# Packing the products of the 8 sample rows into four 32-column groups of the PE array, in a hybrid decoder step

## Chip, cores and metric

One Trainium2 chip, one core. The metric is the device time of one launch in microseconds; runs of the same kernel are compared by their median. TensorE is called PE below, VectorE DVE, ScalarE ACT, GpSimd POOL, and SyncE, which issues nearly all DMAs from one queue, SP.

## What is computed

One layer of a causal decoder for a prompt of 1024 rows (`x_prompt`) and a group of 8 sample rows (`x_sample`, one token of each of 8 sequences at position 8192), with the same weights:

```
h  = LN_in(x)
z  = h @ W_in -> retention q,k,v,gate | dilated-attention q,k,v      (1024 x 3584)
m  = concat(swish(gate) * HeadNorm(Retention(q,k,v)), DilatedAttn(q,k,v)) @ W_out
h1 = LN1(alpha * h + m)
f  = up-projection -> causal depthwise conv (width 3) -> a * gelu(g) -> down-projection
e  = sigmoid(h1 @ W_pg) * (p @ W_pp)
h  = LN2(alpha * h1 + f + e)
```

There are 8 heads of 64 in the retention and 8 of 64 in the attention. A prompt row attends to the prompt under three bands (128, 512 by 4, 2048 by 16). A sample row uses its own cache of 2048 keys and values and its own retention state. The new keys and values, the states and the last up-projected rows are outputs too. Everything is fp32 outside; inside, large products split each operand into an fp16 high part and an fp16 remainder and add three of the four partial products (`PASSES`: high by high, high by low, low by high).

## The kernel before

The program is a row of stages, each with one instruction stream for each engine and semaphores between them: norm_in, retention, attention, samples, mixer, ffn. A stage ends for all engines together, and the next starts after it. The order of the work on each engine is the order in which the code of its stream is written. The prompt has 8 tiles of 128 rows (`t`, `NT` = 8), and the sample rows are a ninth, short tile; `HT` holds the transposed rows in both halves, [128, 2, 8, 1032], with the samples in the last 8 columns. `product` (L80) runs the 3 x 8 matmuls of one output of 512 columns: the rows are the stationary operand, the weights stream.

**retention**: for each pair of heads `p` (4) nine steps `s`, of which the ninth (`s == NT`) is the samples'. PE's step projects tile `s` (L441), then does for older tiles, one to four steps behind, the transposes of q and k (L450), scores (L458), the state, scores by values and the new state (L470 to L474, in one PSUM bank, OB) and the transpose of the result (L479). DVE turns the pairs of the projected tile (`turn_pairs`, L530), and, for the tile three steps behind, updates the state, norms OB (L594) and multiplies by the gate (L598). L470 of a tile waits until L594 of the tile before has read OB. At odd steps DVE also splits weights for the next pair. The loop over the middle pairs is a hardware loop.

**attention**: written out, `g` counts 4 x 9 steps. PE: `project(g)` (L784), `turn(g-1)`, `score(g-2)`, `values(g-5)` (L829). ACT: `soften(g)`, which for the tile three steps back holds two exponentials and two scalings (L847, L855), `split` (L879), `out` (L905), `copy(g)` (L891: the projected tile from PSUM to `QKV`), `turned_high(g-1)`. POOL rotates `QKV` after the copy. SP, for each g: stores of tile g-1 after POOL's rotation (for the samples also to `scratch`), at some steps weight loads, then two DMA transposes of the normed scores (L721) for the tile three steps back. PE's `values` waits for these.

```
    for g in range(NG + LP + 2):
        p, s = divmod(g, NT + 1)
        store(g - 1)
        ...
                load_w(p, c)
        ...
        turn_p(g)
```

**samples**: DVE multiplies queries and cached keys, and a softmax over heads and rows follows, while PE mixes the first 6 tiles of the prompt with W_out (`mix`, through L84). Then PE weighs the cached values: for each of 8 samples b and 3 patterns one fp32 matmul (L1219), with `PBD` [128, 64] as stationary operand, which is zero outside the 8 columns of sample b, so that all 24 add up in one bank, OPS [64, 512]. DVE takes each row's own head out of it (`OWN`), and the result is turned into `MTS`, the samples' mixed rows. The values of a sample have one of four slots; SP loads the next sample into a slot when its three matmuls are done (`v_free`). Half of mix(5) stands between samples 3 and 4, half behind the last.

**mixer**: PE mixes the last two tiles of the prompt and the samples (`mix(2, 0, NB, 0)`, 48 matmuls), then for each of nine tiles turns the rows, runs the gate product (`gate`, 48 matmuls, L84 with `mixer_WG`) and the embedding product (`embed`, 12). ACT and DVE split the ten weight chunks of the gate and the embedding as they arrive; the gate needs eight of them. DVE's `add(t)` (L1482, L1486) finishes a tile.

**ffn**: up-projection, convolution, gelu, down-projection. The samples' part of the down-projection is packed already (`sample_parts`, L1697): the stationary operand holds both halves of the 8 rows, 16 columns, and goes to columns 0, 32, 64 and 96 of the array in turn, for two chunks with the high and the low weights each; the four column groups land in four groups of 32 rows of PSUM, and one matmul with the 0/1 matrix `SUMS` adds them up.

## Time and profile before

| | |
|---|---|
| median of 3 runs | 1564.14 us (1563.77 to 1565.64) |
| the profiled execution, device time | 1564.13 us |
| its span | 1562.3 us |
| PE busy | 1436.7 us (92%) |
| DVE busy | 800.6 us (51%) |
| ACT busy | 457.7 us (29%) |
| POOL busy | 265.9 us (17%) |
| mean granted clock of TensorE | 0.976 |

The profile is of one execution. Its span runs from the first to the last record; times in it are counted from its start. Busy time of an engine is the union of its instructions. A matmul's end is modelled, so the distance from start to start is what one costs in a stream, not the 379 ns given as its mean. An fp32 matmul leaves two records. The stages start at about 70 us (retention), 332 (attention), 574 (samples), 671 (mixer) and 838 (ffn).

### The profile page before, as it was taken

The numbers are of one execution on the slowest core, as the hardware profiler recorded it, in microseconds if no ns is written. First come the engines' busy times: TensorE is split into PE (matmuls) and PEld (weight loads), VectorE is DVE, ScalarE is ACT, GpSimd is POOL, SyncE is SP. The second block draws the span as 40 slices with busy tenths as digits, with TensorE's granted clock in tenths as the row PEclk, the third lists the DMA queues.
The fourth block names the chain that finished last, engine by engine and source line by source line (L and its number), as shares of the span: only waits on it lengthen the run. The fifth ranks groups of instructions, "written<-read, shape, count | busy, mean of one in ns | idle before, by whom it ended". The sixth has DMA issues, their size and how long they took to land. (4 is left out here: it accounts for less than half of the span.)

```text
span 1562.3 us, 24517 instructions
## 1 busy us (share of the span) xinstructions
PE 1436.7 (92%) x8964; PEld 810.6 (52%) x8964; DVE 800.6 (51%) x1611; ACT 457.7 (29%) x743; POOL 265.9 (17%) x330
## 2 busy tenths in 40 slices
PE   1599999969999958999998999999999999999986
PEld 1355555545555533344544666456654566546643
DVE  6656766637567648167533445125541355413547
ACT  2321221127556630022111443004440144302322
POOL 3400101123333305012210110001110011100026
PEclk9999999979999978999999999999999999999998
DMA  7101010026687778341005122012120122101002
GB/s 207 57 27 42 18 50 28 14 60 123 120 156 144 149 164 244 128 148 59 11 1 147 49 78 81 0 40 74 59 69 0 40 81 81 40 0 41 14 14 101
DMA packets 184281, 115.64 MB, mean 74 GB/s; under 512 B 83239, under 2 KB 168055, under 8 KB 183943
## 3 DMA queue, kind: packets, MB, share of 16 engines
q1 hardware_dynamic: 184207, 114.66, 28.3%
q8 instruction: 45, 0.74, 0.2%
q14 instruction: 29, 0.24, 0.0%
HBM read 85.79 MB, written 10.15 MB: 61 GB/s over the span
## 5 line engine op out<-in xcount | busy, mean ns | idle before, releaser
L1647 PE MATMUL PS<-all_HT,all_WS 128*128 128x344 f16 x3168 | 465.1, 310 | 6.5 <-POOLq L73 4.8
L1647 PEld LDWEIGHTS PS<-all_HT,all_WS 128*128 128x128 f16 x3168 | 310.5, 98 | 161.7 <-issue 8.4
L441 PE MATMUL PS<-all_WS,all_HT 128*128 (+3 forms) x864 | 194.4, 382 | 3.8 <-POOLq L73 3.8
L1657 PE MATMUL PS<-all_WS,ffn_HG 128*128 128x512 f16 x608 | 182.3, 379 | 3.6 <-POOL ffn_HG L1807 1.9
L1807 POOL TENSOR_TENSOR ffn_HG<-ffn_PRD,ffn_HG 128x1032 f32 (+1 forms) x22 | 47.2, 2146 | 660.0 <-ACT ffn_HG L1779 660.0
L1767 ACT ACTIVATE ffn_C<-PS,all_CW,all_CWS 128x1032 f32<-128x1032 f32 x44 | 53.1, 1206 | 362.0 <-PE PS L1647 362.0
L784 PE MATMUL PS<-all_WS,all_HT 128*128 128x384 f16 (+1 forms) x864 | 149.2, 330 | 2.9 <-POOLq L73 2.9
L441 PEld LDWEIGHTS PS<-all_WS,all_HT 128*128 128x128 f16 (+1 forms) x864 | 83.7, 97 | 101.3 <-POOLq L73 3.9
L1657 PE MATMUL PS<-ffn_WD,ffn_HG 128*128 128x512 f16 x304 | 115.2, 379 | 0.0
L784 PEld LDWEIGHTS PS<-all_WS,all_HT 128*128 128x128 f16 (+1 forms) x864 | 81.6, 98 | 61.5 <-POOLq L73 3.2
L1657 PEld LDWEIGHTS PS<-all_WS,ffn_HG 128*128 (+1 forms) x608 | 59.4, 98 | 76.9 <-issue 6.0
L84 PE MATMUL PS<-all_WS,all_MT 128*128 128x512 f16 x384 | 88.2, 392 | 11.0 <-DVE all_HRES L1135 7.4
L1864 DVE SCALAR_TENSOR_TENSOR all_HRES<-PS,all_HRES 128x1024 f32 x24 | 29.4, 1225 | 129.1 <-PE PS L1657 128.8
L84 PE MATMUL PS<-mixer_WG,all_HT 128*128 128x512 f16 (+1 forms) x432 | 94.7, 379 | 0.0
L1833 DVE SCALAR_TENSOR_TENSOR all_WS<-ffn_SU,all_WS 128x2048 f16<-128x2048 f32 x21 | 52.0, 2478 | 66.2 <-ACT all_WS L1757 66.2
L1843 DVE TENSOR_SCALAR ffn_UC<-PS 128x10 f32 (+1 forms) x44 | 7.6, 172 | 147.1 <-ACT ffn_CB L1768 147.1
L84 PEld LDWEIGHTS PS<-all_WS,all_MT 128*128 128x128 f16 x384 | 38.1, 100 | 60.3 <-issue 11.2
L84 PEld LDWEIGHTS PS<-mixer_WG,all_HT 128*128 128x128 f16 (+1 forms) x432 | 41.6, 97 | 49.9 <-issue 0.4
L606 POOL TENSOR_TENSOR retention_RSTD<-retention_VE,all_EPSC 128x2 f32<-128x2 f32 x32 | 24.8, 774 | 240.3 <-DVE retention_VE L579 240.3
L847 ACT ACTIVATE attention_PR<-attention_PR,attention_MX 128x128 f32<-128x128 f32 (+7 forms) x64 | 49.1, 767 | 41.2 <-DVE attention_MX L924 41.1
L281 PE MATMUL PS<-all_IDENT,norm_in_HS 128*128 128x128 f32 (+1 forms) x72 | 16.7, 407 | 47.6 <-POOL norm_in_HS L261 47.6
L493 ACT ACTIVATE retention_V<-PS 128x128 f32<-128x128 f32 x32 | 8.9, 278 | 173.0 <-DVE retention_T L530 173.0
(210 smaller groups left out, 1862.9 us busy)
## 6 DMA issues: line engine op xcount, KB each, us to landing
ffn_SU<-in_w_up SPq DMA_DIRECT2D x42, 512.0 KB, 5.0
ffn_SD<-in_w_down SPq DMA_DIRECT2D x22, 512.0 KB, 3.5
all_STG<-in_w_in SPq DMA_DIRECT2D x32, 256.0 KB, 3.2
all_STG<-in_w_in SPq DMA_DIRECT2D x32, 192.0 KB, 3.0
samples_KC<-in_cache_k_win SPq DMA_DIRECT2D x24, 256.0 KB, 3.9
all_HRES<-in_x_prompt SPq DMA_DIRECT2D x8, 512.0 KB, 4.9
out<-attention_QKV SPq DMA_DIRECT2D x64, 64.0 KB, 1.7
all_STG<-in_w_out SPq DMA_DIRECT2D x8, 512.0 KB, 4.0
```

What stands on the lines that cost most here:

```text
L84: mm = nc.tensor.matmul(out[:n], lhs(a, k), w(b, k, c), start=(k == 0 and (a, b) == (0, 0)), stop=(k == kd - 1 and (a, b) == (1, 0)))
L281: last = nc.tensor.transpose(PS[:, 2 * u + k // 4, (k % 4) * P:(k % 4) * P + n], HS[:n, u, k * P:(k + 1) * P], IDENT[:n, :n])
L441: mm = nc.tensor.matmul(Z(s)[:n], HT[:, a, k, s * P:s * P + n], WS[:, slot, b, k, :], start=(k == 0 and (a, b) == (0, 0)), stop=(k == KD - ...
L606: nc.gpsimd.tensor_tensor(RSTD[:], VE[:], EPSC[:], ALU.pow).then_inc(rstd_ready, 1)
L784: mm = nc.tensor.matmul(Z[:n, g % 2, 0:384], HT[:, a, k, s * P:s * P + n], WS[:, p % 2, b, k, 0:384], start=(k == 0 and (a, b) == (0, 0)), ...
L847: nc.scalar.activation(PR[:, x % 4, 0:w], PR[:, x % 4, 0:w], ACT.Exp, scale=-1.0, bias=MX[:, x % 4:x % 4 + 1], accum_out=SUM[:, x % 4:x % ...
L1647: mm = nc.tensor.matmul(U(x)[:, third], UW[:, u, a, k, x * P:(x + 1) * P], HT[:, b, k, third * T3:(third + 1) * T3], start=(k == 0 and (a, ...
L1657: mm = nc.tensor.matmul(DB[u][:rows, half], HG[:, a, l, ds(t * P, rows)], WD[b][:, l, half * 512:(half + 1) * 512], start=(l == 0 and (a, ...
L1767: nc.scalar.activation(C_from(x, 0), U(x), ACT.Identity, scale=CWS[:, 2, ch], bias=CW[:, 3, ch])
L1807: nc.gpsimd.tensor_tensor(HG[:, 1, l, :], PRD[:], HG[:, 0, l, :], ALU.subtract).then_inc(lo_ready, 1)
L1833: nc.vector.scalar_tensor_tensor(UW[:, u, 1].rearrange("p k n -> p (k n)"), SU[:, u].rearrange("p k n -> p (k n)"), S_W, UW[:, u, 0].rearr ...
L1864: nc.vector.scalar_tensor_tensor(HRES[:n, t], DB[u][:n].rearrange("p b n -> p (b n)"), UNDOWN, HRES[:n, t], ALU.mult, ALU.add).then_inc(ad ...
```

## The change

All products whose output rows are the 8 samples are done as ffn's already are: both halves of the rows side by side as a stationary operand of 16 columns (`HTS`, `MTS` in a new layout), two chunks times two halves of the weights in the four column groups at once, 16 matmuls in place of 24 (32 in place of 48); then ACT copies all 128 rows of the partial sums to SBUF and one fp32 matmul with `SUMS` (now loaded once, in norm_in) adds them up. The product of the low parts, which was left out, is thereby included. This holds for the projections in retention and attention, for the mixing and for the gate in the mixer stage. In samples, each of four samples has a column group of its own, with its own 8 probabilities as stationary operand (`PT`, no zeros), the halves of the eight go to two banks, and two small matmuls with a 0/1 matrix (`SEL`) choose the rows. All four slots are reloaded when the whole first half is done. The two helpers that ran retention's pairs in a hardware loop now write them out. In the mixer the gate's packed product stands before embed(7). `dynamic_dma_scratch_size` falls from 1024 to 512.

```diff
+        def product_parts(out, lhs, w, kd):
+            for r in range(kd // 2):
+                for j in range(4):
+                    mm = nc.tensor.matmul(out[32 * j:32 * j + 2 * NB], lhs(2 * r + j // 2), w(j % 2, 2 * r + j // 2),
+                                          start=(r == 0), stop=(r == kd // 2 - 1))
+            return mm
...
@@ norm_in: SP, DVE
+                    sp.dma_start(SUMS[:], c_sum).then_inc(tab_in, 16)
...
+                    dve.wait_ge(lo_ready, BASE + NT + 1)
+                    nc.vector.tensor_copy(HTS[:].rearrange("p k a n -> p a k n"), HT[:, :, :, SEQ:])
...
@@ retention: both loop helpers
-                    with eng.Fori(1, HP - 1) as p:
+                    for p in range(1, HP - 1):
...
@@ retention: PE
                                 if s == NT:
                                     pe.sem_inc(pe_go, 1)
-                                for k in range(KD):
...
+                                    pe.wait_ge(parts_zero, BASE + 1)
+                                    product_parts(Z(s), lambda k: HTS[:, k].rearrange("p a n -> p (a n)"),
+                                                  lambda b, k: WS[:, slot, b, k, :], KD).then_inc(z_parts, 1)
...
                                 nc.tensor.transpose(RB, R[:, t % 2], IDENT[:]).then_inc(r_turned, 1)
+                            if s == NT:
+                                pe.wait_ge(zp_ready, BASE + p + 1)
+                                nc.tensor.matmul(Z(s)[:NB], SUMS[:], ZP[:], start=True, stop=True).then_inc(z_ready, 1)
@@ retention: ACT
+                                if s == NT:
+                                    act.wait_ge(z_parts, BASE + p + 1)
+                                    nc.scalar.activation(ZP[:], Z(s), ACT.Copy).then_inc(zp_ready, 1)
                                 act.wait_ge(halves, BASE + 18 * p + 2 * s + 2)
@@ attention: PE
+                    def add_up(g):
+                        p, s = divmod(g, NT + 1)
+                        if s == NT and 0 <= g < NG:
+                            pe.wait_ge(zp_ready, BASE + p + 1)
+                            nc.tensor.matmul(Z[:NB, g % 2, 0:384], SUMS[:], QKV[:, g % 3], start=True, stop=True).then_inc(z_summed, 1)
...
                             project(g)
+                        add_up(g - 1)
                         turn(g - 1)
@@ attention: ACT
+                        if s == NT:
+                            nc.scalar.activation(QKV[:, g % 3], Z[:, g % 2, 0:384], ACT.Copy).then_inc(zp_ready, 1)
...
+                    def copy_sum(g):
+                        p, s = divmod(g, NT + 1)
+                        if s == NT and 0 <= g < NG:
+                            act.wait_ge(z_summed, BASE + p + 1)
+                            nc.scalar.activation(QKV[:NB, g % 3], Z[:NB, g % 2, 0:384], ACT.Copy, scale=UNSCALE).then_inc(copied, 1)
...
                         soften(g)
+                        copy_sum(g - 1)
                         split(g)
@@ samples: SP, PE, DVE
                         else:
-                            sp.wait_ge(v_free, BASE + b - 3)
+                            sp.wait_ge(pv_done, BASE + 1)
...
+                    def weigh(half):
+                        pe.wait_ge(pt_ready, BASE + 1)
+                        pe.wait_ge(bank_zero, BASE + half + 1)
+                        for j in range(4):
+                            pe.wait_ge(v_in[j], BASE + 48 * (half + 1))
                         for a in range(PAT):
+                            for j in range(4):
+                                b = 4 * half + j
+                                mm = nc.tensor.matmul(OPS[half][32 * j:32 * j + H], PT[:, a, b * H:(b + 1) * H], v_slot(b)[:, a],
+                                                      start=(a == 0), stop=(a == PAT - 1))
+                        mm.then_inc(pv_done, 1)
...
+                    weigh(0)
                     mix(5, (0,))
+                    weigh(1)
                     mix(5, (1,))
+                    pe.wait_ge(ao_ready, BASE + 1)
+                    for half in range(2):
+                        mm = nc.tensor.matmul(APS, SEL[:, half], AO[:, half], start=(half == 0), stop=(half == 1))
+                    mm.then_inc(chosen, 1)
...
+                    dve.wait_ge(chosen, BASE + 1)
                     for twice in range(2):
-                        nc.vector.scalar_tensor_tensor(MIX[:R8, 1, twice], ROW[:R8, 6], SR[:R8, PAT * P:], AO[:R8], ALU.mult,
+                        nc.vector.scalar_tensor_tensor(MIX[:R8, 1, twice], ROW[:R8, 6], SR[:R8, PAT * P:], APS, ALU.mult,
                                                        ALU.add).then_inc(att_done, 1)
@@ mixer: PE, ACT, DVE
                     mix(1, 1, P, (EARLY + 1) * P)
+                    pe.wait_ge(r_ready, BASE + 1)
+                    for c in range(2):
+                        mm = product_parts(M[0][:, c], lambda k: MTS[:, k].rearrange("p a n -> p (a n)"),
+                                           lambda b, k: WS[:, k // 4, b, 2 * (k % 4) + c], KD)
+                    mm.then_inc(parts_done, 1)
                     turn(0)
-                    mix(2, 0, NB, 0)
                     turn_p(0)
+                    add_up(M[0], 1).then_inc(mixed, 1)
...
+                        if t == NT - 1:
+                            gate_parts()
                         embed(t)
+                    add_up(TB, 2).then_inc(gated, 1)
+                    embed(NT)
...
                     for c in range(5, KD):
                         split(c)
+                    copy_parts(M[0], 1)
                     high_p(0)
...
                             low_p(t + 1)
+                        if t == NT - 1:
+                            dve.wait_ge(lo_ready, BASE + NT + 1)
+                            nc.vector.tensor_copy(HTS[:].rearrange("p k a n -> p a k n"), HT[:, :, :, SEQ:]).then_inc(hts_ready, 1)
                         add(t)
```

Two places in the order of the work, each before and after.

ACT in attention, from the sample tile (g = 8) to the next: before, the one copy of the 8 rows.

```order
L891 ACTIVATE attention_QKV<-PS 8x384 [waits attention_v_lo,attention_turned,attention_out_st2,attention_z_ready]
L899 ACTIVATE attention_QKT<-PS 128x256 [waits attention_turned]
L847 ACTIVATE attention_PR,attention_SUM<-attention_PR,attention_MX 128x896 [waits attention_masked]
L855 ACTIVATE attention_P<-attention_PR,attention_RCP 128x768 [waits attention_p_turned3,attention_rcp_ready]
L847 ACTIVATE attention_PR,attention_SUM<-attention_PR,attention_MX 128x896 [waits attention_masked]
L855 ACTIVATE attention_P<-attention_PR,attention_RCP 128x896 [waits attention_p_turned0,attention_rcp_ready]
L905 ACTIVATE all_MT<-PS 128x512 [waits attention_o_ready]
```

The same stretch with the change:

```order
L927 ACTIVATE attention_QKV<-PS 128x384 [waits attention_v_lo,attention_turned,attention_out_st2,attention_z_ready]
L943 ACTIVATE attention_QKT<-PS 128x256 [waits attention_turned]
L883 ACTIVATE attention_PR,attention_SUM<-attention_PR,attention_MX 128x896 [waits attention_masked]
L891 ACTIVATE attention_P<-attention_PR,attention_RCP 128x768 [waits attention_p_turned3,attention_rcp_ready]
L883 ACTIVATE attention_PR,attention_SUM<-attention_PR,attention_MX 128x896 [waits attention_masked]
L891 ACTIVATE attention_P<-attention_PR,attention_RCP 128x896 [waits attention_p_turned0,attention_rcp_ready]
L935 ACTIVATE attention_QKV<-PS 8x384 [waits attention_z_summed]
L949 ACTIVATE all_MT<-PS 128x512 [waits attention_o_ready]
```

The copy of the finished 8 rows moved from the first place to behind the four operations on the scores; in the first place stands the copy of the partial sums.

SP in attention, from the sample tile's stores, with the change; the order is that of before:

```order
L734 DMA out<-attention_QKV 8x128 [waits attention_rotated]
L734 DMA out<-attention_QKV 8x128
L737 DMA scratch<-attention_QKV 8x3x128
L720 DMA all_STG<-in_w_in 128x3x128 [waits attention_w_free]
...
L746 DMA_TRANSPOSE attention_PRT<-attention_P 128x12x128 [waits attention_o_ready,attention_p_lo] x2
L731 DMA out<-attention_QKV 128x128 [waits attention_rotated]
L731 DMA out<-attention_QKV 128x128
L746 DMA_TRANSPOSE attention_PRT<-attention_P 128x14x128 [waits attention_o_ready,attention_p_lo] x2
```

The transposes of tiles 5 (12 blocks of 128) and 6 (14) stand behind the stores of the sample tile.

PE in retention, the sample step and the beginning of the next, before:

```order
L441 MATMUL PS<-all_WS,all_HT 8x512 x24
L450 MATMUL PS<-all_IDENT,retention_QK 128x128 x2
L458 MATMUL PS<-retention_QKT 128x128 x2
L470 MATMUL PS<-retention_STATE,retention_QG 128x128
L472 MATMUL PS<-retention_V,retention_SD 128x64 x2
L474 MATMUL PS<-retention_V,retention_KG 128x128
L479 MATMUL PS<-all_IDENT,retention_R 128x128
```

With the change:

```order
L99 MATMUL PS<-all_WS,all_HTS 16x512 x16
L468 MATMUL PS<-all_IDENT,retention_QK 128x128 x2
L476 MATMUL PS<-retention_QKT 128x128 x2
L488 MATMUL PS<-retention_STATE,retention_QG 128x128
L490 MATMUL PS<-retention_V,retention_SD 128x64 x2
L492 MATMUL PS<-retention_V,retention_KG 128x128
L497 MATMUL PS<-all_IDENT,retention_R 128x128
L500 MATMUL PS<-retention_ZP,all_SUMS 8x512
L459 MATMUL PS<-all_WS,all_HT 128x512 x24
```

The sample projection has 16 matmuls in place of 24, and the finished rows exist only after L500, at the step's end.

## Rows read from the trace of the kernel before

**Rows 1.** Lines of PE: line, operation, shapes, count, busy us, mean ns, idle before.

```profile
L784 PE MATMUL PS<-all_WS,all_HT 128*8 128x384 f16 x96 | 16.3, 326 | 0.0
...
L1219 PE MATMUL PS<-samples_VC,samples_PRD 128*64 128x512 f32 x24 | 10.7, 595 | 0.0
```

**Rows 2.** Timeline of PE, ffn's packed product: start us, length us, instruction.

```profile
1029.02 0.38 PE L1697 MATMUL PS<-all_WS,ffn_HGS 128*16 128x512 f16 x1
...
1029.24 0.38 PE L1697 MATMUL PS<-all_WS,ffn_HGS 128*16 128x512 f16 x1
```

**Rows 3.** Timelines of PE and DVE, retention's first sample step.

```profile
124.10 5.34 PE L441 MATMUL PS<-all_WS,all_HT 128*8 128x512 f16 x24
...
130.16 0.49 PE L470 MATMUL PS<-retention_STATE,retention_QG 128*128 128x128 f32 x2
...
131.27 4.05 PE L441 MATMUL PS<-all_WS,all_HT 128*128 x18
...
127.60 0.58 DVE L594 TENSOR_SCALAR retention_RN<-PS,retention_MV,retention_RSTD 128x64 f32<-128x64 f32 x2
```

**Rows 4.** Timeline of PE, samples: the mixing after its longest wait.

```profile
602.27 23.34 PE L84 MATMUL PS<-all_WS,all_MT 128*128 128x512 f16 x96 [7.35 <-DVE all_HRES L1135]
```

**Rows 5.** Timeline of PE, attention: values of tile 4, then of tile 7 twice.

```profile
385.94 1.03 PE L829 MATMUL PS<-attention_PRT,all_WS 128*64 128x128 f16 x30 [0.25 <-DVE all_MT L978]
...
405.85 2.77 PE L829 MATMUL PS<-attention_PRT,all_WS 128*64 128x128 f16 x48 [3.08 <-issue]
...
461.51 1.53 PE L829 MATMUL PS<-attention_PRT,attention_V 128*64 128x128 f16 x48 [2.06 <-issue]
```

**Rows 6.** Timeline of ACT, attention, around the first sample tile.

```profile
377.92 0.48 ACT L891 ACTIVATE attention_QKV<-PS 8x384 f32<-8x384 f32 x1
...
384.50 0.58 ACT L905 ACTIVATE all_MT<-PS 128x512 f16<-128x512 f32 x1
```

**Rows 7.** Timeline of SP's queue, from the first sample tile's store to tile 7.

```profile
379.99 1.03 SPq L709 DMA_DIRECT2D out<-attention_QKV  x2
...
383.62 4.03 SPq L721 DMA_TRANSPOSE attention_PRT<-attention_P  x2
387.69 1.26 SPq L706 DMA_DIRECT2D out<-attention_QKV  x2
389.51 4.97 SPq L721 DMA_TRANSPOSE attention_PRT<-attention_P  x2
395.08 0.81 SPq L706 DMA_DIRECT2D out<-attention_QKV  x2
...
397.00 7.15 SPq L721 DMA_TRANSPOSE attention_PRT<-attention_P  x2
```

**Rows 8.** Samples: timelines of PE and SP; a window (engines' busy, PEclk, DMA share, GB/s).

```profile
637.37 5.32 PE L1219 MATMUL PS<-samples_VC,samples_PRD 128*64 128x512 f32 x12
...
663.72 5.34 PE L84 MATMUL PS<-all_WS,all_MT 128*128 128x512 f16 x24
...
640.14 3.85 SPq L1065 DMA_DIRECT2D samples_VC<-in_cache_v_win x6
...
655.00:656.00 1.00, 1.00 (x3) 0.27 (x2) 0.00 (x0) 0.00 (x0) 0.00 (x0) 1.00 0.23 90
```

**Rows 9.** Timeline of PE, retention: two transposes, then two fp32 matmuls in two row groups.

```profile
122.17 0.38 PE L450 MATMUL PS<-all_IDENT,retention_QK 128*128 128x128 f32 x2
122.48 0.49 PE L458 MATMUL PS<-retention_QKT 64*128 64x128 f32 x4
```

**Rows 10.** Mixer: timelines of ACT and PE at its start, of PE and DVE at its end.

```profile
702.53 1.06 ACT L1380 ACTIVATE mixer_WG<-mixer_STG 128x1024 f16<-128x1024 f32 x1 [3.02 <-DMA mixer_STG<-in_w_ple_gate]
...
708.37 10.52 PE L84 MATMUL PS<-mixer_WG,all_HT 128*128 128x512 f16 x48
...
819.84 10.52 PE L84 MATMUL PS<-mixer_WG,all_HT 128*8 128x512 f16 x48
...
834.24 1.21 DVE L1486 SCALAR_TENSOR_TENSOR all_HRES<-all_HRES,mixer_R 8x1024 f32<-8x1024 f32 x1
```

More of the change, by code:

```diff
@@ L369, in run @@
                 def run(eng):
-                    with eng.Fori(0, HP - 1) as p:
+                    for p in range(HP - 1):
                         body(eng, p, False)
@@ L1343, in gate, with gate_parts, add_up @@
                         for c in range(2):
-                            mm = product(GB[:, c], n, lambda a, k: HT[:, a, k, t * P:t * P + n],
+                            mm = product(GB[:, c], P, lambda a, k: HT[:, a, k, t * P:(t + 1) * P],
                                          lambda b, k, c: WG[:, b, k, c * 512:(c + 1) * 512], c, KD)
                         mm.then_inc(gated, 1)
+                    def gate_parts():
+                        pe.wait_ge(hts_ready, BASE + 1)
+                        for c in range(2):
+                            mm = product_parts(TB[:, c], lambda k: HTS[:, k].rearrange("p a n -> p (a n)"),
+                                               lambda b, k: WG[:, b, k, c * 512:(c + 1) * 512], KD)
+                        mm.then_inc(parts_done, 1)
+                    def add_up(out, count):
+                        pe.wait_ge(pp_ready, BASE + count)
+                        for c in range(2):
+                            mm = nc.tensor.matmul(out[:NB, c], SUMS[:], PP[:, c * 512:(c + 1) * 512], start=True, stop=True)
+                        return mm
                     def embed(t):
@@ L1961, in constants @@
     gsample = np.tile(np.exp(lg), NB)[:, None]
[L1962 removed]
+    own_head = np.tile(np.concatenate([np.eye(H), np.zeros((32 - H, H))]), (4, 1))
+    own_row = np.zeros((4, 32, 2, 2, 4, H))
+    for j in range(4):
+        for half in range(2):
+            own_row[j, :H, half, half, j] = np.eye(H)
+    own_row = own_row.reshape(P, 2 * NB * H)
     part_sum = np.tile(np.concatenate([np.eye(NB), np.eye(NB), np.zeros((2 * NB, NB))]), (4, 1))
     return [np.ascontiguousarray(a, dtype=f) for a in
[L1965 removed]
+            (np.eye(P), rope_ret, rope_att, decay, gq, kdec, gchunk, mask, gsample, own_head, part_sum, own_row)]
 _INS = ['x_prompt', 'x_sample', 'cache_k_win', 'cache_v_win', 'state_ret', 'state_conv', 'p_prompt', 'p_sample',
```

152 lines of the change are left out of this document (79 added, 73 removed).

## The prediction

> **What bounds the kernel now.** I read the view of windows first: TensorE (PE) is busy for nearly the whole of every stage, so removing PE time looks as if it paid one to one. The view of lines prices what is removed [rows 1]: a sample product of 24 matmuls, 8 rows each, takes as long as one of 128 rows, since a matmul costs its moving columns (16.3 us for the 96 of attention; 21.3 us for the 48 passes over the cached values, of which the row shows half). The question is then, at each of the five places, what ends the wait behind the removed work. For that I read the timelines of the engines around the sample block, and of SP's queue.
>
> **What a packed product costs.** The kernel has packed products already, in ffn [rows 2]: the row of 1029.02 is the first of four that start within 0.01 us, that of 1029.24 the first of the next four, 0.215 us later. So 16 matmuls of 512 columns take 4 x 0.215 = 0.86 us in place of 24 x 0.215 = 5.16, 16 of 384 columns 0.65 in place of 3.9, and 32 take 1.72 in place of 10.3. The new sum is one fp32 matmul over 512 columns: two passes of 10.7/24 = 0.44 us [rows 1], 0.87 together (0.65 for 384 columns). It stands behind a copy of ScalarE (ACT) of about 0.5 us.
>
> **Retention, four blocks.** The packed product is 4.3 us shorter, but DVE is not faster. In the block of sample rows PE next needs the OB bank, free once DVE has normed the tile before [rows 3]: 127.60 + 0.58 = 128.2. Now PE comes there at 130.16; after the change at 124.10 + 0.86 + 0.8 = 125.75, so it waits 2.5 us. From there 1.1 us to the end of the block (130.16 to 131.27, as now) and 0.87 for the sum: 130.3 in place of 131.27, 1.0 us gained. DVE gets the sample rows at 130.4 and not right behind the projection (124.10 + 5.34 = 129.4); the next tile's projection (5.2 us) covers that. Three blocks gain 2.9. The fourth has no projection behind it: the stage drains along DVE, which starts its sample rows 0.65 us later. Sum -2.2. The new waits of 2.5 us can lower PE's clock. After a wait of 7.35 us, 96 matmuls took 23.34 us [rows 4] and not 96 x 0.215 = 20.6, so a fall costs up to 2.7 us; after the wait of 2.06 us in [rows 5] the 48 matmuls took 1.53 us, as fast as elsewhere, after one of 3.08 us 2.77. I take one fall in three blocks, +2.0 (none: 0; all: 6). The unrolled loops add only code; PE shows no gap at the turns of the loop, so I cost them at nothing. **Retention: -0.2.**
>
> **Attention, four blocks.** Here two things eat the 3.9 - 0.65 - 0.65 = 2.6 us. First, PE's values of tile 4, one step after the sample block, wait already for ACT and DVE (0.25 us at 385.94 [rows 5]), whose chain of exponentials does not depend on the sample block. So PE only waits there for longer. Second, the finished sample rows come later, and SP stands in line behind them. Now ACT copies them at 377.92 [rows 6], GpSimd rotates them, and SP stores them at 379.99 [rows 7], 2.07 us after the copy began. With the change, that first copy only brings the partial sums; the second stands in ACT's order behind the four large operations of the next tile, which end at 384.50 [rows 6], 0.4 earlier at best. So SP's store starts at 384.1 + 2.07 = 386.2, +6.2 us. Behind that store in SP's order are the four weight loads and then the DMA transposes of tile 5. Those start at 383.62 now, with no pause since the store, and at 389.8 then. The pauses of SP after them, 388.95 to 389.51 and 395.89 - 0.81 - 394.48 = 0.6 us, are used up; the last pair (tile 7), at 397.00 now, starts 5.0 us later. PE's values of tile 7 wait for this pair even now: 3.08 us at 405.85, 2.06 at 461.51 [rows 5]. They come 5.0 us later in the first group; in the second and third I get +4.5 and +4.2 from the same steps, with the pauses that SP has there. PE runs without a gap from there to the next sample block, so nothing of it is regained. In the first group PE will have waited 4 us earlier (values of tile 5) and found its clock again by tile 7, where it is low now (2.77 us for the row at 405.85, 1.53 at 461.51): -1.9 with the projection behind it. The last group ends in a drain: ACT has the second copy (0.45 us) in its chain, and the last loads of W_out stand behind the late store; 0.5 to 2.5, taken as 1.5. **Attention: 3.1 + 4.5 + 4.2 + 1.5 = +13.3.** If SP caught up wholly it would be -5.5 (see the rivals); if PE's clock fell before the other tile 7s too, +17.
>
> **Cached values.** The 24 fp32 matmuls take 20.8 us from 637.37, with a half of mixing (5.2) in their middle and one at their end, from 663.72 [rows 8]. How do fp32 matmuls in different groups overlap? The trace has the question for groups of rows, [rows 9]: four passes of 128 columns (two matmuls) end 0.49 us after the first began, two passes after 0.38 with one step of 0.107. Four in sequence would need 0.38 + 2 x 0.107 = 0.59; 0.49 is one step fewer: the first pass of the second matmul runs beside the second pass of the first. So n matmuls take n + 1 passes, and 12 take 13 x 0.44 = 5.7 us in place of 10.4. But now a slot is refilled only when all four of the first half are done: loads start at 643.3, not at 640.14, and PE's second half waits for all twelve. Now 4.2 MB, 3.1 of them cached values, take from 641 to 655.7 [rows 8]: 11.9 us for the values, from issue. Second half at 655.2 (mixing hides 5.2 of that, 7 us stay bare), 5.7 us, 2.7 for the clock after such a wait, mixing 5.2, and a new tail: choosing matmuls and the two DVE operations on att_done now stand behind the mixing, 1.2 us. End 670.0, now 663.72 + 5.2 = 668.9. **+1.1.** Without any overlap (10.4 twice) it would be +10.5. The Trainium skill (TensorE: Matmul & The Clock Gate, Measured speedup vs the span model) gives packed matmuls one duration plus about 4 ns for each further tile. By that rule twelve would take three durations, 2.6 us, and this stage would give -5.1 (663.8); [rows 9] show another thing for fp32 with its two passes, and the sum goes by them.
>
> **Mixer.** At its start the sample product hides under the splitting of the gate weights: gate(0) needs eight, and ACT waits 3.02 us for DMA before the eighth, at 702.53 [rows 10]. PE turns the first tile only after the packed product, 1.8 us later than now, and ACT's and DVE's splits behind that move by 1.5. ACT's copy of the partial sums stands behind the eighth split, at 702.53 + 1.06 + 1.5 = 705.1; PE, idle for 9 us, adds at half clock (3.4 us) and reaches gate(0), with the turning of the next tile, at 711.0 in place of 708.37: +2.6. At the end there is nothing to hide behind: embed(7) ends at 819.84, and 10.4 for the gate, 2.6 for the embedding and DVE follow, up to 834.24 + 1.21 [rows 10]. After the change: 1.55 us of wait for the copy of HTS (DVE makes it only behind low_p), 1.8 for the packed gate, then embed(7), add_up 1.7, embed(8) 2.6 and DVE's 2.5: 830.0. -5.4. **-2.8.**
>
> norm_in's added copy and load end before ACT does, and ffn only loses a load. **Sum: -0.2 + 13.3 + 1.1 - 2.8 = +11.4.** The profiled execution took 1564.13 us, like the median of the runs (1564.14): **1575.5 us**. A measurement of this kernel tells 0.2% (3.1 us) from no change.
>
> **Rivals.**
> - *SP catches up.* Transposes take 7.15 us for the pair of tile 7 and 4.03 for that of tile 5 [rows 7], though four thirds as large. If the length comes from what else is under way, a queued pair may take 3 us; then tile 7 is served before 405.85, the waits of 3.08 and 2.06 us and the low clock (1.7) vanish, and attention gives -5.5: 1564.1 - 7.3 = **1556.8**. It decides from 5 us regained between the store and tile 7. Against it: the pairs get longer where loads and stores stand between them, and these stay. 0.21. If two thirds are regained, no change is measured: 0.12.
> - *All PE time counts:* four times 3.4 and 2.6, 9.4 at the cached values (20.8 - 11.4), 13.8 in the mixer, together -47: **1517**. It needs every wait above to be wrong. 0.05.
> - *fp32 groups side by side*, as the rule quoted: 6.2 us less than my sum, **1569.3**. Speaks for it: f16 does so. 0.12.
> - *fp32 groups one after another*, as column groups may differ from row groups: +9.4 on my sum, **1584.9**. 0.08.
>
> **Numbers.** My forecast has 0.42; with the last two rivals slower has 0.62, no change 0.12, faster 0.26. The range leaves out the second rival and part of the outermost: 1556 to 1585.
>
> **What would show it.** Right: SP's sample store 12 us after PE's sample block began and not 6; tile 5's transposes behind it; PE idle 4 us before the values of tile 5; ACT and DVE unchanged up to there; a wait of some 2.5 us at L470's successor in retention; some 7 us before the second half of the cached values; 9 us idle before the mixer's first sum. Wrong: values of tile 7 no later than now, or passes of fp32 groups that start together.

## The result, and the profile after

The changed kernel takes 1576.59 us (median of 4 runs, 1573.3 to 1576.87), the kernel before 1564.18 us in the same comparison: ratio 1.0080, 95% interval 1.0065 to 1.0094. It is slower by 12.4 us; 11.4 were forecast. The profiled execution has a span of 1574.5 us, 12.2 more than before. PE is busy for 1398.5 us, 38.2 us less than before: the removed work is gone, and the time is not.

Where the time came and went is read by stage. A stage starts with PE's first matmul in it; the table takes these starts from PE's timeline (70.34, 332.58, 574.04, 671.13 and 837.79 before; 69.80, 338.99, 596.79, 686.84 and 849.88 after).

| stage | before, us | after, us | difference | forecast |
|---|---|---|---|---|
| norm_in | 70.3 | 69.8 | -0.5 | 0 |
| retention | 262.2 | 269.2 | **+7.0** | -0.2 |
| attention | 241.5 | 257.8 | **+16.3** | +13.3 |
| samples | 97.1 | 90.1 | **-7.0** | +1.1 |
| mixer | 166.7 | 163.0 | -3.6 | -2.8 |
| ffn to the end | 724.5 | 724.6 | +0.1 | 0 |

So the total was right by luck, by errors of opposite sign: retention was underrated by 7.2 us, attention by 3.0, and samples overrated in cost by 8.1.

The view of windows of the changed kernel, retention, attention and samples; the columns are the stretch, its length, the busy time of PE, PE's weight loads, DVE, ACT and POOL, the granted clock, the DMA share and GB/s:

```profile
69.80:339.00 269.20, 245.58 (x1321) 131.59 (x1322) 162.97 (x608) 50.16 (x157) 25.42 (x32) 0.94 0.11 31
339.00:596.80 257.80, 209.18 (x2057) 127.73 (x2058) 147.03 (x380) 143.79 (x293) 78.74 (x208) 0.92 0.63 128
596.80:686.80 90.00, 72.77 (x352) 30.66 (x352) 47.87 (x48) 3.26 (x7) 23.32 (x10) 0.94 0.62 191
```

And of the kernel before:

```profile
70.30:332.60 262.30, 250.20 (x1345) 134.72 (x1346) 164.52 (x608) 48.66 (x153) 24.75 (x32) 0.98 0.11 32
332.60:574.00 241.40, 216.23 (x2080) 131.93 (x2080) 147.37 (x380) 142.27 (x289) 77.88 (x208) 0.94 0.69 137
574.00:671.10 97.10, 87.54 (x348) 35.76 (x349) 46.73 (x51) 3.26 (x7) 24.70 (x11) 0.95 0.60 176
```

In retention PE is busy 4.6 us less and idle 11.5 us more, at a lower granted clock (0.94, was 0.98). In attention it is idle 23.5 us more.

**Attention.** SP's queue behind the first sample tile, the answer to [rows 7]:

```profile
391.47 0.66 SPq L734 DMA_DIRECT2D out<-attention_QKV  x2
392.17 0.30 SPq L737 DMA_DIRECT2D scratch<-attention_QKV  x1
392.51 3.21 SPq L720 DMA_DIRECT2D all_STG<-in_w_in  x4
395.83 4.35 SPq L746 DMA_TRANSPOSE attention_PRT<-attention_P  x2
...
407.79 6.91 SPq L746 DMA_TRANSPOSE attention_PRT<-attention_P  x2
```

PE's sample block began at 379.65, so the store starts 11.8 us behind it (6.2 before), the transposes of tile 5 follow it, and those of tile 7 start at 407.79. The late copy is on ACT's timeline (answers to [rows 6]): the copy of the finished rows stands behind the four large operations.

```profile
383.67 0.47 ACT L927 ACTIVATE attention_QKV<-PS 128x384 f32<-128x384 f32 x1
...
388.80 1.03 ACT L891 ACTIVATE attention_P<-attention_PR,attention_RCP 128x896 f16<-128x896 f32 x1
389.73 0.46 ACT L935 ACTIVATE attention_QKV<-PS 8x384 f32<-8x384 f32 x1
```

And PE's timeline from the sample block on, the answer to [rows 5]: the values of tile 4 wait 1.72 us for DVE, those of tile 5 5.61 us for the transposes, and run, with the projection behind them, at half clock.

```profile
379.65 0.83 PE L99 MATMUL PS<-all_WS,all_HTS 128*16 128x384 f16 x16
...
391.54 1.03 PE L864 MATMUL PS<-attention_PRT,all_WS 128*64 128x128 f16 x30 [1.72 <-DVE all_MT L1023]
...
402.40 2.13 PE L864 MATMUL PS<-attention_PRT,all_WS 128*64 128x128 f16 x36 [5.61 <-issue]
404.47 5.63 PE L813 MATMUL PS<-all_WS,all_HT 128*128 128x384 f16 x24
...
416.81 1.53 PE L864 MATMUL PS<-attention_PRT,all_WS 128*64 128x128 f16 x48 [0.27 <-issue]
```

**Retention.** PE's timeline of the second sample step, the answer to [rows 3]:

```profile
185.33 1.04 PE L99 MATMUL PS<-all_WS,all_HTS 128*16 128x512 f16 x16
...
189.56 0.77 PE L488 MATMUL PS<-retention_STATE,retention_QG 128*128 128x128 f32 x2 [2.40 <-DVE retention_RN L619]
190.12 0.95 PE L490 MATMUL PS<-retention_V,retention_SD 128*128 128x64 f32 x4
...
191.75 1.88 PE L500 MATMUL PS<-retention_ZP,all_SUMS 128*8 128x512 f32 x2
193.56 6.57 PE L459 MATMUL PS<-all_WS,all_HT 128*128 128x512 f16 x24
```

The wait of 2.40 us is the one forecast (2.5). But the clock falls behind it: the sum takes 1.88 us (1.02 at full clock, experiment 5), and the next projection 6.57 in place of 5.34.

**Samples.** The first round of four matmuls over the cached values, and the first of the second half, on PE's timeline (answers to [rows 8]); rounds follow each other every 0.43 us, so these are the two passes of 0.43 us each, in four column groups within 0.02 us:

```profile
658.82 0.60 PE L1272 MATMUL PS<-samples_VC,samples_PT 128*8 128x512 f32 x2
658.83 0.60 PE L1272 MATMUL PS<-samples_KC,samples_PT 128*8 128x512 f32 x2
659.25 0.60 PE L1272 MATMUL PS<-samples_VC,samples_PT 128*8 128x512 f32 x2
659.26 0.60 PE L1272 MATMUL PS<-samples_KC,samples_PT 128*8 128x512 f32 x2
...
661.51 5.35 PE L84 MATMUL PS<-all_WS,all_MT 128*128 128x512 f16 x24
674.58 1.03 PE L1272 MATMUL PS<-samples_VC,samples_PT 128*8 128x512 f32 x2 [7.72 <-DMA samples_KC<-in_cache_v_win]
```

The half takes 661.51 - 658.82 = 2.69 us, and PE then waits 7.72 us for the refill.

**Mixer.** PE's timeline at the start, behind the first two tiles:

```profile
721.35 3.58 PE L1411 MATMUL PS<-mixer_PP,all_SUMS 128*8 128x512 f32 x4 [8.87 <-ACT mixer_PP L1481]
724.86 1.19 PE L1379 MATMUL PS<-all_IDENT,all_HRES 128*128 128x128 f32 x8
725.89 10.52 PE L84 MATMUL PS<-mixer_WG,all_HT 128*128 128x512 f16 x48
```

### The profile page after: what moved, and what is told of

It reads as the page before. It is cut to its first block and busy times, and to the rows that moved or that the text cites. A ratio compares the mean times of both kernels' runs of the same rounds, so it can differ in the third digit from the quotient of the medians.

```text
span 1574.5 us, 24008 instructions
## 1 busy us (share of the span) xinstructions
PE 1398.5 (89%) x8896; PEld 792.2 (50%) x8896; DVE 802.6 (51%) x1611; ACT 462.5 (29%) x753; POOL 266.0 (17%) x329
## 5 line engine op out<-in xcount | busy, mean ns | idle before, releaser
L459 PE MATMUL PS<-all_WS,all_HT 128*128 128x512 f16 x768 | 174.3, 384 | 3.8 <-POOLq L73 3.8
L813 PE MATMUL PS<-all_WS,all_HT 128*128 128x384 f16 x768 | 134.8, 334 | 2.9 <-POOLq L73 2.9
L459 PEld LDWEIGHTS PS<-all_WS,all_HT 128*128 128x128 f16 x768 | 75.7, 99 | 95.3 <-issue 9.8
L813 PEld LDWEIGHTS PS<-all_WS,all_HT 128*128 128x128 f16 x768 | 74.2, 100 | 55.8 <-issue 5.4
L84 PE MATMUL PS<-mixer_WG,all_HT 128*128 128x512 f16 x384 | 84.2, 379 | 0.0
L555 DVE TENSOR_TENSOR retention_T<-PS,norm_in_R_ROPE 128x256 f32<-128x256 f32 (+1 forms) x72 | 27.3, 418 | 67.8 <-PE PS L459 39.3
L84 PEld LDWEIGHTS PS<-mixer_WG,all_HT 128*128 128x128 f16 x384 | 37.5, 98 | 43.5
```

The costliest lines, as they stand in the source:

```text
L84: mm = nc.tensor.matmul(out[:n], lhs(a, k), w(b, k, c), start=(k == 0 and (a, b) == (0, 0)), stop=(k == kd - 1 and (a, b) == (1, 0)))
L459: mm = nc.tensor.matmul(Z(s)[:n], HT[:, a, k, s * P:s * P + n], WS[:, slot, b, k, :], start=(k == 0 and (a, b) == (0, 0)), stop=(k == KD - ...
L555: nc.vector.tensor_tensor(dst[:n].rearrange("p (g e) -> p g e", e=E // 2), z, ROPE[:n, s, j].unsqueeze(1).broadcast_to([n, 8, E // 2]), AL ...
L813: mm = nc.tensor.matmul(Z[:n, g % 2, 0:384], HT[:, a, k, s * P:s * P + n], WS[:, p % 2, b, k, 0:384], start=(k == 0 and (a, b) == (0, 0)), ...
```

## Experiments

Stage times below are taken as in the table above, from the profile of each kernel; ratios are to the kernel before, measured in the same comparison. Kernels with the same code in a stage as the changed one differ there by up to 3.2 us: retention 266.5 to 269.6, attention 256.1 to 259.1, samples 90.1 to 92.9, mixer 160.8 to 163.2. So smaller differences of a stage are read from single rows.

**1. The late copy alone, in the kernel before.**

```diff
                         soften(g)
+                        if g >= 1 and (g - 1) % (NT + 1) == NT:
+                            copy(g - 1)
                         split(g)
                         out(g - LP - 1)
-                        copy(g)
+                        if g % (NT + 1) < NT:
+                            copy(g)
```

> The kernel before, all products as they were; only ACT's copy of the attention's sample tile stands behind the four large operations of the next tile, as the second copy of the changed kernel does. Theory of the queue (SP stands behind the late rows, the DMA transposes of tiles 5 and 7 behind SP): the sample tile's store starts some 6.5 us later, PE's values of tile 5 wait some 4 to 6 us, attention takes 253 to 258 us in place of 241.5, the kernel 1576 to 1581 us. Rival (the shorter product itself, with PE's waits and its clock, costs the 16 us): attention stays at 241.5, the kernel at 1564 us.

Measured: 1580.97 us, ratio 1.012 (1.0096 to 1.0144); attention 259.2 us (1.2 above the expected range), all other stages as before (retention 262.1, samples 98.2, mixer 166.7). The store starts 12.4 us behind the sample block, 6.2 later than before. In the kernel before, with no product packed, PE's values of tile 5 now wait as in the changed one:

```profile
384.86 1.03 PE L829 MATMUL PS<-attention_PRT,all_WS 128*64 128x128 f16 x30 [0.61 <-DVE all_MT L981]
...
394.90 2.13 PE L829 MATMUL PS<-attention_PRT,all_WS 128*64 128x128 f16 x36 [4.78 <-issue]
```

One copy of 8 rows, moved by one step, costs 17.7 us. That is the whole loss of attention (16.3); the 1.4 us between the two are less than the 3 us by which the stage differs with the same code.

**2. SP's order in the changed kernel.**

```diff
-                        store(g - 1)
+                        late = g >= 1 and (g - 1) % (NT + 1) == NT
+                        if not late:
+                            store(g - 1)
                         ...
                         turn_p(g)
+                        if late:
+                            store(g - 1)
```

> The changed kernel; only SP's stores of the attention's sample tile stand behind the two DMA transposes of the same step instead of ahead of them. Theory of the queue: attention falls from 257.8 to about 237 us (the 241.5 of before less most of 5.5), the kernel from 1576.6 to about 1556 us; the waits of 5.6 us before the values of tile 5 are gone. Rival (the transposes of tile 5 are late for another reason, the softened scores or the queue's transfers): no more than 3 us less, 1574 us or more.

Measured: 1559.71 us, ratio 0.9981 (0.9967 to 0.9995); attention 240.3 us. ACT's late copy is still there. SP now turns tile 5 at 387.67, stores at 391.55, and PE does not wait for tile 5:

```profile
384.76 2.30 SPq L720 DMA_DIRECT2D all_STG<-in_w_in  x4
387.67 3.83 SPq L746 DMA_TRANSPOSE attention_PRT<-attention_P  x2
391.55 1.04 SPq L734 DMA_DIRECT2D out<-attention_QKV  x2
```

```profile
391.06 1.03 PE L868 MATMUL PS<-attention_PRT,all_WS 128*64 128x128 f16 x30 [1.71 <-DVE all_MT L1027]
...
396.24 1.20 PE L868 MATMUL PS<-attention_PRT,all_WS 128*64 128x128 f16 x36
...
410.75 2.77 PE L868 MATMUL PS<-attention_PRT,all_WS 128*64 128x128 f16 x48 [2.86 <-issue]
```

17.5 us of attention are back (the stage was expected at 237, the kernel at 1556). The stage is only 1.1 us shorter than before packing: the waits for DVE before the values of tile 4 and for the transposes before those of tile 7 hold what PE has gained.

**3. The other remedy: ACT's and PE's order.** SP as in the changed kernel; `add_up(g)` stands at the end of its own step, ACT copies the partial sums ahead of `soften`, and the finished rows where the one copy was.

```diff
-                        add_up(g - 1)
...
                         values(g - LP)
+                        add_up(g)
...
+                        if g % (NT + 1) == NT:
+                            copy(g)
                         soften(g)
-                        copy_sum(g - 1)
                         split(g)
                         out(g - LP - 1)
-                        copy(g)
+                        if g % (NT + 1) < NT:
+                            copy(g)
+                        copy_sum(g)
```

> The changed kernel, SP's order untouched; in attention PE adds the sample tile's partial sums at the end of the same step (not in the next), ACT copies the partial sums ahead of the tile's four large operations and the finished rows where the kernel before has its only copy. Theory of the queue: the finished rows come as early as before, SP's store starts some 6 us after PE's sample block, no wait of 5.6 us before the values of tile 5; attention 240 to 243 us in place of 257.8, the kernel 1559 to 1562 us. Rival (the second copy costs ACT's chain its length in any place, and PE waits for it as well): attention above 246, the kernel above 1565.

Measured: 1564.85 us, ratio 1.0012 (0.9999 to 1.0025); attention 244.8. The store starts at 383.28, 6.5 us behind the sample block, and the wait before the values of tile 5 is gone: the theory holds. Attention and kernel end between the two expectations (the profiled execution, at 1560.09 us, is the fastest of ten). The stage takes 4.5 us more than in experiment 2. Two rows hold 1.8 of them: the values of tile 4 wait 2.14 us (1.71 in experiment 2), and in the drain the scores of the last tile wait 3.71 us for DVE (2.33 there). That it is the second copy which lengthens ACT's chain fits them, but where the rest of the 4.5 us goes was not traced.

**4. Retention as it was.** The 24 matmuls of 8 rows, without copy and sum, in the changed kernel.

> The changed kernel with retention's sample projection as before: 24 matmuls of 8 rows, no copy, no sum. If retention's 7.0 us come from the packed product (waits of 2.4 us, the lower granted clock behind them, and the late rows in the drain), retention takes 262.2 us again in place of 269.2 and the kernel 1569.6 us. Rival (the unrolled pairs or the new loads cost it): retention stays near 269, the kernel near 1576.

Measured: 1569.41 us, ratio 1.0042 (1.0028 to 1.0056); retention 262.7 us. Unrolled pairs and added loads cost nothing that can be told (retention was 262.2 before); packing cost the 7 us.

**5. The sum in the middle of the step.**

```diff
                                 mm.then_inc(scored, 1)
+                            if s == NT and kind != "after":
+                                pe.wait_ge(zp_ready, BASE + p + 1)
+                                nc.tensor.matmul(Z(s)[:NB], SUMS[:], ZP[:], start=True, stop=True).then_inc(z_ready, 1)
                             q, t = tile_at(s, 3, p, kind)
...
-                            if s == NT:
-                                pe.wait_ge(zp_ready, BASE + p + 1)
-                                nc.tensor.matmul(Z(s)[:NB], SUMS[:], ZP[:], start=True, stop=True).then_inc(z_ready, 1)
```

> The changed kernel with retention's sum matmul in the middle of PE's sample step, ahead of the wait for DVE's norm (behind the scores of tile 6), and not at the step's end. The sum (0.87 us) then lies inside the wait of 2.4 us. Theory A (the place of the sum costs: 1.9 us in each of three blocks at the lower clock, and DVE's late sample rows in the drain): retention 269.2 less 5.6 less about 3.5, 260 us, the kernel 1567.5. Theory B (the waits and the clock they lower cost, wherever the sum stands): the step still waits until DVE has normed, the clock falls as now, retention 265 to 268, the kernel 1573 or more.

Measured: 1563.41 us, ratio 1.0003 (0.9993 to 1.0013); retention 256.9 us, 12.3 less than with the sum at the end, 5.3 less than before packing. Theory A, and more than it counted: the wait for DVE's norm shrinks to 1.33 us, and the clock does not fall behind it.

```profile
185.12 1.02 PE L481 MATMUL PS<-retention_ZP,all_SUMS 128*8 128x512 f32 x2
187.47 0.46 PE L491 MATMUL PS<-retention_STATE,retention_QG 128*128 128x128 f32 x2 [1.33 <-DVE retention_RN L619]
...
188.55 5.34 PE L459 MATMUL PS<-all_WS,all_HT 128*128 128x512 f16 x24
```

**6. The cached values loaded ahead.** `VH` is a place of its own in `HT`, with semaphores of its own.

```diff
-                return (VC if b % 4 < 2 else KC)[:, b % 2]
+                return VH[:, b - 4] if b >= 4 else (VC if b < 2 else KC)[:, b % 2]
...
-                        else:
-                            sp.wait_ge(pv_done, BASE + 1)
```

> The changed kernel; the cached values of samples 4 to 7 get a place of their own (the transposed rows HT are not needed in this stage) and are loaded right behind those of samples 2 and 3, not after the first half's products. Theory (PE's wait of 7.7 us and the low clock behind it, 1.5 us, are the price of refilling all four slots at once): both vanish, the stage takes about 81 us in place of 90, the kernel 1567.5 us. Rival (the loads collide with those of samples 2 and 3, and the first half starts late instead): 86 us or more, 1572.5 or more.

Measured: 1566.5 us, ratio 1.0021 (1.001 to 1.0032); samples 79.7 us, 10.4 less than in the changed kernel, 17.4 less than before. SP issues the twelve loads at 643.91, and PE goes from the mixing straight into the second half, at full clock:

```profile
664.00 2.76 PE L1272 MATMUL PS<-all_HT,samples_PT 128*8 128x512 f32 x24
```

**7. Matmuls sample by sample**, three in a row in one column group, then the next group.

> The changed kernel; the 12 fp32 matmuls over the cached values of one half are issued sample after sample (three in a row in one column group) and no longer in turns over the four column groups. If matmuls of different groups run side by side only when they follow each other, the half takes about 4 x 3 x 0.86 = 10.3 us less the overlap at three borders, 8 to 10 us in place of 2.7; if the array looks further ahead in its queue, 3 to 5 us. The kernel: 1576.6 us plus 5 to 14 us by the first, plus at most 3 by the second.

Measured: 1585.92 us (one run); samples 98.3 us. The first half takes 662.77 to 668.05 = 5.28 us: between the two expectations, closer to the second (the kernel's 9.3 us more fall into the first, for the reason given below). So it is twice the 2.69 of matmuls in turns, and half of the 10.4 that 12 such matmuls take in one group [rows 8]. The records show how the groups overlap; samples 0 and 1 read `VC`, samples 2 and 3 `KC`:

```profile
662.77 2.32 PE L1272 MATMUL PS<-samples_VC,samples_PT 128*8 128x512 f32 x8
664.51 0.60 PE L1272 MATMUL PS<-samples_KC,samples_PT 128*8 128x512 f32 x1
...
665.79 0.59 PE L1272 MATMUL PS<-samples_VC,samples_PT 128*8 128x512 f32 x1
```

The first pass of sample 2 (664.51) starts 1.3 us before the last of sample 1 (665.79), which stands ahead of it in the program. The 24 passes start in twelve steps of 0.43 us, 1, 1, 2, 2, 3, 3, 3, 3, 2, 2, 1 and 1 at a time. That is what comes out if each group begins one matmul (two passes) behind the group before it and not three: three matmuls, and three times a lag of one, are 6 x 0.87 = 5.2 us. (The stage lost 8.2 us, more than 2 x 2.6, since the second half ran at half clock for longer: 8.07 us for 4.03.)

**8. The mixer's start.** PE turns the first tile ahead of the packed product, and ACT copies ahead of the eighth split.

```diff
+                    turn(0)
                     pe.wait_ge(r_ready, BASE + 1)
...
                     mm.then_inc(parts_done, 1)
-                    turn(0)
...
-                    for c in range(5, KD):
-                        split(c)
+                    split(5)
+                    split(6)
                     copy_parts(M[0], 1)
+                    split(7)
```

> The changed kernel; in the mixer stage PE turns the first tile ahead of the samples' packed product and not behind it, and ACT copies the partial sums ahead of the eighth weight chunk's split (for which it waits 4.1 us for a DMA) and not behind it. Theory (PE's idle 8.9 us and the sum at half clock, 3.6 us, stand on the way to the first gate product): the first gate product starts 4 to 6 us earlier, the stage takes 157 to 159 us in place of 163, the kernel 1571 to 1573 us. Rival (the gate product waits for the weight chunks anyhow, and PE's longer wait only lowers its clock): 161 us or more, 1575 or more.

Measured: 1571.91 us, ratio 1.0055 (1.0039 to 1.0072); mixer 158.1 us, 4.9 less. PE waits 3.41 us before the sum, not 8.87, and the first gate product starts 32.6 us into the stage, not 39.0; 1.4 of these 6.4 us are lost again before the second gate product, which starts 15.4 us after the first and not 14.0.

**9. All four moves together** (2, 5, 6 and 8).

> The changed kernel with four moves together: retention's sum ahead of the norm's wait, SP's sample stores behind the DMA transposes in attention, the cached values loaded ahead, and the two moves at the mixer's start. If the four are independent the gains add: 1576.6 less 12.3 (retention) less 17 (attention) less 9 (samples) less 5 (mixer) = 1533 us. If what one frees is waited for elsewhere, 1540 or more.

Measured: 1536.21 us, ratio 0.9823 (0.9807 to 0.984); retention 256.6, attention 240.8, samples 84.3, mixer 158.8. That lies between the two expectations. The gains of retention, attention and the mixer add up; samples take 4.6 us more than in experiment 6, most of it in one wait ahead of PE's fifth tile of mixing, which the moves don't touch: 8.22 us for DVE, 4.92 in experiment 6.

**10. The same without packing in attention** (one copy, no sum, SP's order as before).

> The kernel with all four moves (1536.2 us), but attention's sample projection as in the kernel before: 24 matmuls, one copy, no sum, SP's order as before. Theory (PE's gain in attention is eaten by its wait for ACT and DVE before the values of tile 4 and 7): packing is worth at most 1 us there, the kernel takes 1535 to 1538 us. Rival (packing is worth the 2.6 us of a block four times once the queue is mended): 1541 us or more.

Measured: 1533.73 us, ratio 0.9811 (0.9795 to 0.9827); attention 241.3 us, 0.5 more than packed. Packed, the four products are 3.2 us shorter each, less 0.8 for the sum; these 10 us of PE time are worth half a microsecond of the stage at most, and that is less than the stage differs with the same code. The kernel as a whole is the faster one without packing here, 1533.7 against 1536.2 (1.3 below the expected range): samples (82.1 against 84.3) and mixer (157.7 against 158.8) have the same code in both and make up more than this.

**11. HTS copied earlier at the mixer's end**, on top of experiment 9: DVE copies right behind `low(t + 1)` of the ninth tile.

> The kernel with all four moves (1536.2 us), and at the mixer's end DVE copies the samples' transposed rows (HTS) right behind the low part of the ninth tile, 9 us earlier, not behind low_p. PE's wait of 1.28 us before the gate's packed product goes: the kernel takes 1535 us. By the rival (DVE's last chain ends the stage, whatever PE does) no change, 1536.2.

Measured: 1531.74 us, ratio 0.9804 (0.9782 to 0.9826), the fastest; PE's wait of 1.28 us is gone. From the second gate product to ffn the mixer takes 108.60 us, and 109.94 to 110.04 in every other kernel that has the packed gate: the edit gives 1.3 us, and the rival is out. The whole stage doesn't show it as sharply, since its start varies (157.8 us; 158.8 in experiment 9, 157.7 in experiment 10, both with the wait). Most of the 4.5 us lies in samples (80.9 in place of 84.3), where the two have the same code, so it is no effect of this edit.

## Why the prediction was right in its time, and wrong in three of its terms

**Attention, right in the queue.** "So SP's store starts at 384.1 + 2.07 = 386.2, +6.2 us": it starts 11.8 us behind the sample block, 12.4 were forecast. "The last pair (tile 7) ... starts 5.0 us later": counted from the sample block, 407.79 - 379.65 = 28.1 against 397.00 - 373.82 = 23.2, +5.0; the values of tile 7 likewise, +5.1. Experiments 1 and 2 show the cause from both sides. The step that was too small is the price of PE's wait in the groups: from sample block to sample block 60.2, 59.6 and 57.2 us, in place of 56.7, 54.1 and 52.2, so +3.5, +5.5 and +5.0 where +3.1, +4.5 and +4.2 stood; and the drain cost 2.8, not 1.5.

The forecast laid this price on the wait before the values of tile 7, and PE's rows lay most of it on tile 5. The values of tile 5 start 5.5, 5.0 and 3.9 us later in their groups, and the half clock behind that wait adds 2.5, 1.6 and 1.4 by tile 6. Before tile 7 PE then waits only 0.27, 0.99 and 0 us (3.08, 2.06 and 0.17 before). The third group shows it best, with no wait left at tile 7:

```profile
520.67 2.13 PE L864 MATMUL PS<-attention_PRT,all_WS 128*64 128x128 f16 x36 [4.01 <-issue]
...
533.65 1.53 PE L864 MATMUL PS<-attention_PRT,all_WS 128*64 128x128 f16 x48
```

So the late store acts through the next pair of transposes behind it, and the wait there, with the half clock behind it, uses up what PE had waited for further on.

**"SP catches up", wrong.** From the store to tile 7 SP regained 0.7 us of 5.7 (1.2 were forecast from its pauses, 5 by the rival): the pair of tile 7 took 6.91 us and the pair of tile 5 4.35, against 7.15 and 4.03.

**Retention, wrong in two terms.** "I take one fall in three blocks, +2.0 (none: 0; all: 6)": the clock fell in all three. The blocks with the projection behind them took 0.8, 2.3 and 0.8 us more than before, where 1.0 less without a fall was forecast, so the three falls cost 3.9 + 2.9 = 6.8 us: 1.8, 3.3 and 1.8, where the forecast had at most 2.7 each. The row by which I took one in three, the wait of 2.06 us in attention [rows 5], was not near enough. Of 18 such waits of 2.4 us (three in each of six kernels that have the sum at the step's end), 17 lowered the clock, and of 12 waits of 1.33 us (three in each of four kernels with the sum ahead of the wait) none. The other term: "The fourth has no projection behind it: the stage drains along DVE, which starts its sample rows 0.65 us later". From the fourth sample block to the end of the stage it was 27.55 us in place of 23.92, +3.6. DVE's timeline after, and before, shows it: DVE starts the sample rows 7.9 us behind the block (311.44) and not 5.4 (308.66), after a wait for the sum, which stands behind PE's own wait for DVE's norm.

```profile
319.31 0.74 DVE L555 TENSOR_TENSOR retention_T<-PS,norm_in_R_ROPE 8x256 f32<-8x256 f32 x2 [3.73 <-PE PS L500]
```

```profile
314.10 0.74 DVE L530 TENSOR_TENSOR retention_T<-PS,norm_in_R_ROPE 8x256 f32<-8x256 f32 x2 [1.28 <-PE PS L441]
```

I had added the sum behind an unhindered step; with the wait of 2.13 us and the half clock this row alone comes 2.4 us later, and more of the matmuls behind it run at half clock. Experiment 5 takes both away and gives 12.3 us.

**Cached values, wrong in one term.** "n matmuls take n + 1 passes, and 12 take 13 x 0.44 = 5.7 us": they took 2.69. [rows 9] had led me to a stagger of one pass; four column groups run with both their passes side by side, as the rival of that name had it (chance 0.12). And [rows 9] didn't show a stagger. I had worked it out from the length of a merged row, 0.49 us. The view of windows of the kernel before, with L458 alone, counts the passes under way (the first number with an x is PE's):

```profile
122.45:122.55 0.10, 0.07 (x2) 0.07 (x2) 1.00 0.00 0
...
122.60:122.65 0.05, 0.05 (x2) 0.05 (x4) 1.00 0.00 0
122.65:122.70 0.05, 0.05 (x3) 0.05 (x4) 1.00 1.16 328
```

Two passes are under way by 122.55 and the third comes only behind 122.65, where a stagger with steps of 0.107 us would have had three by 122.60. So the two row groups start their first passes together, and that was to be seen before the forecast. The rule of the Trainium skill (TensorE: Matmul & The Clock Gate, Measured speedup vs the span model) was right where I went by [rows 9]: it gives three durations, and the trace shows three times two passes, 6 x 0.43 = 2.6 us. The refill was costed well: 11.9 us forecast, 12.9 measured from the first issue (661.64) to the second half (674.58), 7.72 us of it bare against 7. The second half took 4.03 us, at low clock for its first three rounds, where 5.7 + 2.7 stood. The two halves and the load together make 3.0 + 4.4 - 1.0 = 6.4 us of the 8.1; 1.3 more came ahead of the first half, where the same code varies as much from kernel to kernel.

**Mixer, right.** The start cost 1.8 us (+2.6 forecast), with the 8.9 us of idle time that were forecast as 9, and the sum at half clock (3.58 us, 3.4 forecast); from gate(0) to ffn it was 129.42 before and 123.99 after, -5.4 as forecast.

Had I taken the rule for the fp32 groups, the other errors would have been left alone, and the forecast, 1569.3, would have been 7 us too low. The right total says little here; the stage table does.

## What to carry to other kernels

A product that is packed with a sum behind it gives its result later, even where its matmuls end sooner: before packing, follow the result on every engine (who copies, stores and turns it, and what stands behind that in the same queue), not the matmuls. Here one copy of 8 rows that had moved by one step on ACT cost 17.7 us through SP's queue, and one change of order in that queue gave 17.5 back; with four such moves the packed kernel takes 0.982 of the time before (experiment 9), though in one of its stages packing is still worth half a microsecond at most. A hole that shorter work opens is best filled with the new work itself, as the sum is in experiment 5: the same matmul costs 1.88 us and a slow clock behind the hole, and nothing in it. And where a reading rests on how single instructions overlap, ask for their starts and not for the length of a merged row.

## What the runs showed of the hardware

- Waits of PE of 2.4 us lowered its granted clock from 1.00 to 0.50 (2.4 to 1.2 GHz) in 17 of 18 cases; waits of 1.33 us did in none of 12. Ahead of both stands the sample step's product and small fp32 matmuls, ahead of the shorter ones the sum as well.
- fp32 matmuls (two passes) in four column groups run side by side when issued in turns: 12 of 512 columns in 2.69 us. Issued three in a row to a group they take 5.28 us, and a pass of a later group starts before passes that were issued ahead of it (664.51 against 665.79 in experiment 7); in one group 12 take 10.4.
- A refill of 3.1 MB in twelve transfers took 12.9 us from the first issue to the matmul that needed the last; issued ahead, beside other work (experiment 6), it made PE wait for nothing.
